# Sixteen of 128 first keys taken out of three tiles' expert gathers and worked out densely

## The chip, the cores and the metric

One core of one Trainium2 chip. The time is the device time in microseconds of one launch. Before: 2917.52 us, the median of three runs (2913.64 to 2918.01).

## The reference

A hybrid attention block over 1024 tokens of width 1024, and behind it a PEER layer, which is what matters here. For each token, 8 heads score 128 first keys and 128 second keys, take the best 16 of each, form the 256 sums, and keep the best 16. Each names one of 128 × 128 = 16384 experts; an expert is a row `u` and a row `v` of 1024 floats.

```python
top_s, pos = lax.top_k(cand_s, PEER_TOPK)
idx = jnp.take_along_axis(cand_i, pos, axis=-1)      # i1 * 128 + i2
g = jax.nn.softmax(top_s.astype(jnp.float32), axis=-1)
u = expert_u[idx]
act = jax.nn.gelu(jnp.einsum('thkd,td->thk', u, tb).astype(jnp.float32), approximate=False)
coef = (g * act).astype(tb.dtype)
return jnp.einsum('thk,thkd->td', coef, expert_v[idx])
```

Then the residual sum and a last RMSNorm. Everything is float32. The expert number is `i1 * 128 + i2`, so all experts of the sixteen highest first keys (112 to 127) have numbers from 14336 on: they are the last 2048 rows of the table.

## The kernel before

The 1024 tokens are eight tiles of 128, worked in eight **blocks** b = 0 to 7. Block b does the experts of tile b, and beside it all other work of tile b + 1 (attention, output product, norm, queries, keys, top-k), and, in blocks 0 to 4, parts of the stick-breaking attention of later tiles. Blocks 5 and 6 have no such attention, block 7 no next tile.

**Experts of a block.** 128 gathers, one for each of the 128 (head, rank) slots, in 64 groups of two (`GRP` = 2, `NG` = 64). A gather is an indirect DMA on GpSimd (L763): 128 rows of `experts`, a row being `u` and `v` side by side, 8192 bytes, into one of nine slots of `r_uv` (64 tokens × 2 ranks over the 128 partitions). The slot order is `SLOT`; a gather waits until TensorE has used the slot's former row (`rows_used`). For every row:

- VectorE multiplies `u` with the normed token and sums (L1437, "the dot"), in place over the `u` half; once a group it builds the gated identity (L1421) from the softmax gates.
- ScalarE applies Gelu to the group's dots (L1020) and writes the gated identity times that over the first 64 columns of the row (L1023).
- TensorE multiplies this 128 × 64 diagonal with `v` in two halves of 512 columns (L1877) and sums over the whole block in PSUM banks 0 and 1. That frees the slot.

All four engines run their own list of instructions, written out by hand: in each engine's `experts_of(b, ...)` the loop runs over the groups n, and tables `at`, `at_own` say which step of the next or of the own tile stands behind which group. VectorE has the largest of these lists: in groups 1 to 25 the second four heads' top-k of the own tile (`top`, `pick`, `gate`, `routed`), in groups 2 to 17 the attention steps of the next tile (`rope`, `mask`, `norm`, `h2`, `hn`), in 27 to 52 the first four heads' top-k of the next tile. A `look` step has three instructions over 800 columns (L1206, L1208, L1209).

TensorE's steps for the next tile are in groups 1 to 29: L1773 is the output product, L1795 the queries, L1816 the keys. L1684 spreads a gain vector over PSUM by eight products (`spread_gain`).

**Finish of a tile.** In block b + 1, group 0: VectorE adds the experts' sum to `h2cur` (`add_rows`, L1399). Group 1: ScalarE's square with its sum, Ln and Exp (L1012, L788, L789; the table is loaded at L784). Group 3: VectorE's Newton step (L1060 to L1064) and the scaling (L1409), then SyncE stores the tile. Group 7: VectorE copies the next residual row into `h2cur` (L1450). After group 63 of block 7 the same chain stands at the end of the kernel.

**SyncE** issues all other DMAs in one list: stored and loaded pieces of the projections, attention keys and values, the rows of the next tile, the finished tiles. From block 5 on it has little to do.

Of the kernel before, what the change touches and what calls it, by code (L numbers as in the profile page):

```python
# [26 lines left out]
P = 128  # L27
# [189 lines left out]

C_ID, C_TRI, C_ONES, C_M01, C_MNEG, C_PERM = (P * i for i in range(6))
# [30 lines left out]
def block_program(nc, x, meta, w_chunks, w_v, consts, rope_cs, w_out, sinks, w_query, keys_t, experts, out):  # L249
    with ExitStack() as ctx:  # L250
# [36 lines left out]
        keysT = grid(sb("keysT", PH * NKEYS), PH)  # L287
# [23 lines left out]
        stream_chunk = grid(sb("stream_chunk", D)[:, :], DC)  # L311
# [72 lines left out]

        def chunk_home(c):

            return wchunk[CHUNK_HOME[c]]
# [31 lines left out]
        lvm_dram = scratch("lvm_dram", [META, PAIRS, P])  # L419

# [42 lines left out]
        hs_in = sem("hs_in")  # L463
        gid_ready = sem("gid_ready")
# [8 lines left out]
        passed = {}  # L473
        for name in ("pe", "act", "dve", "pool", "sp"):
            passed[name] = sem("passed_" + name)
# [13 lines left out]
        def _(sp_eng):  # L489
# [108 lines left out]

            def piece_moves(n0, n1):
# [15 lines left out]
            def late_moves(b, first):  # L615
# [18 lines left out]
                for n, (u, last) in enumerate(LATE_LOADS[first]):  # L634
# [4 lines left out]
                    if n == 2:  # L639
                        if pairs == 2:  # L640
                            if b < STREAM_BLOCKS:
                                stored(pieces_by(at))
                            load_queries(1)

                        gate(e, "sp", qT_done, PH * b + 2 * PH)
                    if n >= LKB:

                        gate(e, "sp", lw_used, ub + LATE_LOADS[first][n - LKB][1] + 1)
# [23 lines left out]
            def store_block(b):  # L672
                e.wait_ge(out_ready, b + 1)
                e.dma_start(out[P * b:P * b + P, :], h2cur[:, :]).then_inc(out_done, 16)

            for b in range(NT):
                if b:
# [3 lines left out]
                    e.wait_ge(out_done, 16 * b)  # L681
# [10 lines left out]
                elif b + 2 < NT:  # L692

                    gate(e, "sp", mix_done, 4 * b + 8)
                    load_window(b + 2)
            for h in range(2):
                e.wait_ge(out_ready, NT + h)
                cols = slice(D // 2 * h, D // 2 * h + D // 2)
                e.dma_start(out[P * (NT - 1):P * NT, cols], h2cur[:, cols]).then_inc(out_done, 16)
# [4 lines left out]
        def _(pool):  # L704
# [40 lines left out]
            def gathers_of(b, late=None):  # L745
                for k in range(K):
# [14 lines left out]
                    elif SLOT[G] in (2, 3):  # L761
                        gate(pool, "pool", proj_summed, NP)
                    g.indirect_dma_start(uv[:, SLOT[G], :], None, experts,  # L763
                                         bass.IndirectOffsetOnAxis(idx[b % 2][:, k:k + 1], 0)
                                         ).then_inc(rows_in[SLOT[G]], 16)
# [10 lines left out]
        def _(act):  # L776
# [229 lines left out]

            def finish(b):
# [4 lines left out]
                link(a.activation(qT_v[:, :], h2cur[:, :], ACT.Square, accum_out=r4[:, 0:1]))  # L1012
# [4 lines left out]
            def experts_of(b, more, late=None):  # L1017
                for n in range(NG):
# [8 lines left out]
                    if n == 1 and b:  # L1027
# [3 lines left out]
                    if n in (own_at if b else own_first):  # L1031
                        tile_step((own_at if b else own_first)[n], b)
                    if late is not None and (late_units(late, n - WEIGHTS[late]) or late_units(late, n - LOGS)):
# [13 lines left out]
        def _(dve):  # L1047
# [166 lines left out]
            def tile_step(step, t):  # L1214
# [30 lines left out]
                elif step == "pT":  # L1245
                    for i in range(2):
# [35 lines left out]
                elif step == "hn":  # L1282
                    dve.wait_ge(h2_squared, t + 1)
                    polish(r3[:, 1:2], r3[:, 0:1], D)
                    dve.wait_ge(gain_spread, max(1, 2 * t))
# [23 lines left out]
                elif step[0] == "routed":  # L1309
# [7 lines left out]
                    spread(gates[t % 2], gn, TOPK * h0, TOPK * h1).then_inc(routed, 1)  # L1317
# [25 lines left out]
                elif step[0] == "look":  # L1343
                    h = step[1]

# [49 lines left out]
            def add_rows(b):  # L1395

                dve.wait_ge(rows_used, K * b + K + NB)
                hg = h2cur[:, :].rearrange("p (a n) -> p a n", a=2)
                v.tensor_tensor(hg, ps[:, 0:2, :], hg, ALU.add).then_inc(h3_ready, 1)  # L1399

            def finish(b):

                dve.wait_ge(h3_squared, b + 1)
                polish(r4[:, 1:2], r4[:, 0:1], D)
                dve.wait_ge(gain_spread, 2 * b + (3 if b < NT - 1 else 2))
                hg = grid(h2cur[:, :], 2)
                for h in range(2 if b == NT - 1 else 1):
                    part = slice(h, h + 1) if b == NT - 1 else slice(0, 2)
                    v.scalar_tensor_tensor(out=hg[:, part, :], in0=hg[:, part, :], scalar=r4[:, 1:2],  # L1409
                                           in1=ps[:, 4 + part.start:4 + part.stop, :], op0=ALU.mult, op1=ALU.mult  # L1410
                                           ).then_inc(out_ready, 1)

# [567 lines left out]
```

## Time and profile before

| | |
|---|---|
| median of three runs | 2917.52 us |
| profiled execution, span | 2918.2 us (0.7 above the median) |
| busy: PE, DVE, POOL, ACT | 2207.9, 2182.3, 1308.8, 1144.8 us |
| moved by DMA | 1155.22 MB, mean 396 GB/s |
| of it by the gathers' queue | 1073.81 MB |
| mean granted TensorE clock | 0.880 |

The blocks by the first dot of each (start of L1437's instruction 0, 128, 256 ...): block 0 from 175.0, block 1 from 546.1, then 905.6, 1264.5, 1598.6 (block 4), 1933.4, 2261.1, 2586.7 (block 7), and the last dot ends at 2907.5.

How to read it: times are microseconds from the first instruction. PE is TensorE, PEld its weight loads, DVE VectorE, ACT ScalarE, POOL GpSimd, SP SyncE. A group of instructions is named by its line, and "idle before" is the time its engine stood idle just before it, with what ended that. DMA share is the mean busy share of the sixteen DMA engines. Busy matmuls overlap, so their busy sum is less than count times mean.

### The profile page before, as it was taken

What the parts mean: (1) busy time and instruction counts of PE and PEld (TensorE: products, weight loads), DVE (VectorE), ACT (ScalarE), POOL (GpSimd) and SP (SyncE); (2) the same over time, 40 slices, a digit from 0 to 9 for tenths busy, and PEclk for the clock granted to TensorE, in tenths of its full rate; (3) what the DMA queues carried; (4) which work ended last, traced back from release to release, by engine and by line L of the source; (5) the groups of instructions that cost most, each with busy time, mean ns of one, the idle gap of its engine ahead of it and who ended that gap; (6) DMA issues with size and microseconds to landing.
All of it is one profiled execution on the core that took longest, in us unless ns stands there. A gap on an engine that the chain in (4) does not pass through costs nothing.

```text
span 2918.2 us, 30160 instructions
## 1 busy us (share of the span) xinstructions
PE 2207.9 (76%) x9182; PEld 944.6 (32%) x9182; DVE 2182.3 (75%) x5506; ACT 1144.8 (39%) x2673; POOL 1308.8 (45%) x1126
## 2 busy tenths in 40 slices
PE   9988888788887988867877777867755775565555
PEld 7564532345333453323322232212311231111111
DVE  4179887786867867689786988779776987668555
ACT  3523277433563335632575327733212321121111
POOL 0024355443554445544565445644444444444442
PEclk9999998999999999988998899988877898777778
DMA  8279999999999999999999999999999999999997
GB/s 324 91 290 406 382 404 420 407 412 389 416 387 419 413 392 411 391 415 420 420 419 408 421 419 403 416 417 418 421 409 422 420 403 420 417 422 406 422 421 322
DMA packets 189328, 1155.22 MB, mean 396 GB/s; under 512 B 23072, under 2 KB 40416, under 8 KB 57712
## 3 DMA queue, kind: packets, MB, share of 16 engines
q0 software_dynamic: 147456, 1073.81, 89.6%
q1 hardware_dynamic: 41712, 79.49, 7.3%
q8 instruction: 74, 1.21, 0.2%
q14 instruction: 86, 0.70, 0.1%
HBM read 1138.21 MB, written 15.01 MB: 395 GB/s over the span
## 4 chain that ended last, share of the span: by engine, by line
DMA 34%; PE 26%; DVE 24%; ACT 9%; issue 5%; POOL 1%; another core or an unknown queue 0%; ACTq 0%; DVEq 0%; SPq 0%; POOLq 0%
DMA r_uv<-in_experts,r_wk 34%; PE ps L1877 12%; DVE r_uv L1437 11%; PE ps L1547 4%; ACT r_uv L1023 2%; PE ps L1795 2%; PE ps L1541 2%; ACT L1020 2%; DVE r_wk L1208 1%; DVE r_wk L1206 1%; DVE r_wk L1209 1%; ACT L784 1%; PE ps L1773 1%; POOL r_uv L763 1%; PE ps L1563 1%
## 5 line engine op out<-in xcount | busy, mean ns | idle before, releaser
L763 POOL DMA_INDIRECT r_uv<-in_experts,r_wk x1024 | 1202.8, 1175 | 1416.7 <-PE ps L1877 1207.6
L1877 PE MATMUL ps<-r_uv 128*64 128x512 f32 x4096 | 1229.8, 733 | 679.0 <-ACT r_uv L1023 662.6
L1437 DVE CUSTOM_DVE_ANT_0 r_uv<-r_uv,hnrep 128x1024 f32<-128x1024 f32 x1024 | 1255.9, 1241 | 555.9 <-DMA r_uv<-in_experts,r_wk 541.0
L1877 PEld LDWEIGHTS ps<-r_uv 128*64 128x64 f32 x4096 | 290.2, 157 | 1424.2 <-ACT r_uv L1023 955.8
L1020 ACT ACTIVATE r_wk<-r_wk 128x2 f32<-128x2 f32 x512 | 103.8, 203 | 1455.5 <-DVE r_wk L1437 1426.4
L1023 ACT ACTIVATE r_uv<-gid,r_wk 128x64 f32<-128x64 f32 x684 | 200.6, 340 | 11.6 <-ACT r_wk L1020 0.2
L1020 ACT ACT_TABLE_LOAD x138 | 177.1, 1283 | 2.4
L784 ACT ACT_TABLE_LOAD x117 | 150.1, 1283 | 6.1 <-PE ps L1753 1.8
L1547 PE MATMUL ps<-r_uv,stream_chunk 128*128 128x256 f32 x560 | 134.0, 394 | 4.7 <-DMA stream_chunk<-in_w_chunks 4.7
L1795 PEld LDWEIGHTS ps<-r_wk,r_wq 128*128 128x128 f32 x1024 | 120.2, 193 | 37.4 <-issue 36.8
L1795 PE MATMUL ps<-r_wk,r_wq 128*128 128x128 f32 x1024 | 129.3, 281 | 0.3 <-ACT r_wk L940 0.3
L1547 PEld LDWEIGHTS ps<-r_uv,stream_chunk 128*128 128x128 f32 x560 | 106.2, 195 | 50.6 <-issue 36.9
L1557 PE MATMUL ps<-r_wk 64*128 64x256 f32 (+2 forms) x384 | 110.0, 419 | 4.3 <-DMA r_wk<-lkv_dram 1.9
L1421 DVE TENSOR_TENSOR gid<-cst,r_wk 128x128 f32<-128x128 f32 x342 | 106.4, 311 | 0.0
L1023 ACT ACTIVATE r_uv<-cst,r_wk 128x64 f32<-128x64 f32 x340 | 99.7, 340 | 5.7
L714 POOL TENSOR_TENSOR r_wk<-r_wk 128x512 f32<-128x512 f32 (+1 forms) x64 | 85.0, 1328 | 31.3 <-PE ps L1569 30.6
L1563 PE MATMUL ps<-r_wk,cst 128*128 128x512 f32 (+2 forms) x184 | 99.0, 621 | 0.0
L1437 DVE DVE_READ_ACCUMULATOR2_ANT r_wk<- 128x1 f32 x1024 | 83.5, 81 | 0.0
L712 POOL COPY r_wk<-r_wk 128x256 f32<-128x256 f32 x32 | 21.0, 657 | 134.7 <-PE ps L1566 106.0
L1557 PEld LDWEIGHTS ps<-r_wk 64*128 64x128 f32 (+1 forms) x384 | 45.8, 178 | 84.5 <-issue 83.8
L1569 PE MATMUL ps<-r_wk,cst 128*128 128x512 f32 (+2 forms) x152 | 72.0, 556 | 0.0
L1208 DVE TENSOR_TENSOR r_wk<-r_wk 128x800 f32<-128x800 f32 (+1 forms) x65 | 63.5, 978 | 2.2
(181 smaller groups left out, 2206.2 us busy)
## 6 DMA issues: line engine op xcount, KB each, us to landing
r_uv<-in_experts,r_wk POOLq DMA_INDIRECT x1024
stream_chunk<-in_w_chunks SPq DMA_DIRECT2D x30, 512.0 KB
r_wk<-lkv_dram SPq DMA_DIRECT2D x36, 256.0 KB
r_uv<-in_x SPq DMA_DIRECT2D x8, 512.0 KB, 10.6
r_wo<-in_w_chunks SPq DMA_DIRECT2D x8, 512.0 KB, 11.4
r_wk<-in_x SPq DMA_DIRECT2D x8, 512.0 KB
r_wo<-in_w_out SPq DMA_DIRECT2D x8, 512.0 KB, 9.5
r_wq<-in_w_query SPq DMA_DIRECT2D x8, 512.0 KB, 6.4
```

Source lines behind the costliest of these rows:

```text
L763: g.indirect_dma_start(uv[:, SLOT[G], :], None, experts, bass.IndirectOffsetOnAxis(idx[b % 2][:, k:k + 1], 0)).then_inc(rows_in[SLOT[G]], 16)
L784: a.preload_act_table_set("natural_log_exp_and_others")
L1020: link(a.activation(actv[:, GRP * n:GRP * n + GRP], actv[:, GRP * n:GRP * n + GRP], ACT.Gelu))
L1023: a.activation(uv[:, SLOT[K * b + k], 0:HALF], gid[(NG * b + n) % 3][:, k % GRP, :], ACT.Copy, scale=actv[:, k:k + 1]).then_inc(diag_ready, 1)
L1208: link(v.tensor_tensor(eq, eq, ci[:, h, 0:among].unsqueeze(1).unsqueeze(1).to_broadcast(every), ALU.mult))
L1421: v.tensor_tensor(gid[m % 3][:, :, :], ident64.unsqueeze(1).to_broadcast([P, GRP, HALF]), gates[b % 2][:, GRP * n:GRP * n + GRP].unsqueeze ...
L1437: v.tensor_tensor_reduce(uv[:, slot, 0:D], uv[:, slot, 0:D], hnrep[:, k % GRP, :], 1.0, 0.0, ALU.mult, ALU.add, actv[:, k:k + 1]).then_inc ...
L1547: last = t_.matmul(piece_sums(i, width), w[:, c, :], tokens, start=c == 0, stop=c == DC - 1)
L1557: t_.matmul(bank(u, r, c0, r0=r0)[:, h, :], k[rows, 0:r], q[rows, c0:GW], start=opens, stop=False, skip_group_check=True).then_inc(lz_half ...
L1563: last = t_.matmul(bank(u, r, c0), negtri[0:r, 0:r], sp[0:r, :, c0:GW], start=False, stop=not own and rest == GW, skip_group_check=True)
L1795: last = t_.matmul(into, wq[:, c, P * h:P * h + P], hnT[:, c, :], start=c == 0, stop=c == DC - 1)
L1877: last = t_.matmul(ps[HALF * j:HALF * j + HALF, i, :], uv[:, slot, 0:HALF], uv[:, slot, D + 512 * i:D + 512 * i + 512], start=n == 0, stop ...
```

## The change

For tiles 4, 5 and 6 (`DENSE`), the experts of the last sixteen first keys (`NA` = 16, numbers from `CUT` = 14336) leave the gathers and are worked out for all 384 tokens at once.

- **Gathers** of blocks 4 to 6 get a bound of `CUT - 1`: a row beyond it isn't an error and is left out. The slot keeps what it held. The gates of such rows are set to 0 (one more small VectorE instruction in `routed`), and the dots of these blocks write their products elsewhere (`spent`, the unused `stage` and `stream_chunk`) so that a slot's `u` half stays finite.
- **Kept for later**, by SyncE: the normed columns of tiles 4 to 6 (`hn_dram`, 0.5 MB each), their expert numbers and gates (`route_dram`, 2 × 64 KB each), and instead of the finished tiles 4 and 5 the partial sums (`part_dram`). The finish of tiles 4 to 6 (squares, Newton step, scaling, store) moves to the end of block 7. Tile 6's partial sum stays in `h2cur`; tile 7 stays in `hs`.
- **Block 6:** SyncE loads the columns again and, through four buffers, sixteen blocks of `u` (512 KB each, transposed on the host: `dense_u`). From group 30, a half block a group, TensorE forms 128 experts × 384 tokens (eight products a block), and ScalarE applies Gelu (`late_act`). In groups 56 to 63 the three tables of expert number and gate are split into first and second key and turned.
- **Block 7, groups 0 to 33:** for each token, the gates are put in the place of their expert: a mark "second key equals column" (128 × 128) times gates by first key (128 × 16), one product a token. VectorE makes the marks of tiles 5 and 6 eight tokens at a time (32 units), ScalarE those of tile 4 four tokens at a time (32 steps of four squares and a Relu); VectorE multiplies the counted gates into `late_act`, twelve times.
- **Block 7, groups 35 to 60:** SyncE loads sixteen blocks of `v` (the first four already in block 6), TensorE sums all into six PSUM banks, 96 products of 512 columns. Groups 61 to 63: the three tiles are added, squared, scaled, and stored ahead of tile 7.
- Six pairs of idle products near the end (L1883) go.

```diff
+NA = 16
+CUT = (NKEYS - NA) * NKEYS
+DENSE = (4, 5, 6)
+DB = 4
+UNIT = 8
+STEP = 4
+SHARE = 16
+DOTS_AT = 30
+TABLE_SPLIT_AT, TABLE_TURN_AT, TABLE_KEEP_AT = (56, 58, 60), 62, 63
+ACT_STEPS_AT = {h: h for h in range(P // STEP)}
+DVE_UNITS_AT = {u: u for u in range(2 * NU_OF)}
+ACT_TIMES_AT = {COUNTED // STEP * (m + 1) + 1: m for m in range(P // COUNTED)}
+DVE_TIMES_AT = {CHUNK_U * m + CHUNK_U + 1: m for m in range(2 * NU_OF // CHUNK_U)}
+SUMS_AT = [35 + 13 * v // 16 for v in range(2 * NA)]
+CLOSE_ADD_AT, CLOSE_SQUARE_AT, CLOSE_SCALE_AT = 61, 62, 63
...
@@ SyncE
+            def load_dense(n):
+                if n >= DB:
+                    if n - DB < NA:
+                        e.wait_ge(dots_done, n - DB + 1)
+                    else:
+                        e.wait_ge(dense_used, n - DB - NA + 1)
+                a = n % NA
+                if n < NA:
+                    e.dma_start(dense[n % DB].rearrange("p (c k) -> p c k", c=DC), dense_u[a]).then_inc(chunk_in[n % DB], 16)
+                else:
+                    e.dma_start(dense[n % DB], experts[CUT + P * a:CUT + P * a + P, D:2 * D]).then_inc(chunk_in[n % DB], 16)
...
@@ GpSimd
+                    if b in DENSE:
+                        g.indirect_dma_start(uv[:, SLOT[G], :], None, experts,
+                                             bass.IndirectOffsetOnAxis(idx[b % 2][:, k:k + 1], 0),
+                                             bounds_check=CUT - 1, oob_is_err=False
+                                             ).then_inc(rows_in[SLOT[G]], 16)
...
@@ ScalarE
+                for k in range(STEP):
+                    last = a.activation(mark[:, k, :], key_iota, ACT.Square, scale=-1.0, bias=turned_of[0][:, 1, at + k:at + k + 1])
+                link(last)
+                a.activation(mark, mark, ACT.Relu, scale=-2.0, bias=1.0).then_inc(act_marked, 1)
...
@@ VectorE
+                v.tensor_tensor(mark, key_iota.unsqueeze(1).to_broadcast([P, UNIT, P]),
+                                turned_of[i][:, 1, k0:k0 + UNIT].unsqueeze(2).to_broadcast([P, UNIT, P]), ALU.is_equal)
+                link(v.tensor_tensor(share, block_iota.unsqueeze(1).to_broadcast([P, UNIT, NA]),
+                                     turned_of[i][:, 0, k0:k0 + UNIT].unsqueeze(2).to_broadcast([P, UNIT, NA]), ALU.is_equal))
+                v.tensor_tensor(share, share, turned_of[i][:, 2, k0:k0 + UNIT].unsqueeze(2).to_broadcast([P, UNIT, NA]), ALU.mult
+                                ).then_inc(dve_marked, 1)
...
+                            if b in DENSE and k >= 2:
+                                dve.wait_ge(dotted, K * b + k - 1)
-                            v.tensor_tensor_reduce(uv[:, slot, 0:D], uv[:, slot, 0:D], hnrep[:, k % GRP, :], 1.0, 0.0,
+                            v.tensor_tensor_reduce(spent[k % 2] if b in DENSE else uv[:, slot, 0:D], uv[:, slot, 0:D],
+                                                   hnrep[:, k % GRP, :], 1.0, 0.0,
...
@@ TensorE
+            def count_tokens(bank, at, mark, share):
+
+                for k in range(mark.shape[1]):
+                    last = t_.matmul(ps[:, bank, NA * (at + k):NA * (at + k) + NA], mark[:, k, :], share[:, k, :],
+                                     start=True, stop=True)
+                return last
...
+                for j in range(ND):
+                    last = t_.matmul(ps[:, 2 + 2 * j + i, :], late_act[:, a_, P * j:P * j + P],
+                                     dense[n % DB][:, 512 * i:512 * i + 512], start=a_ == 0, stop=a_ == NA - 1)
```

## Rows read from the trace of the kernel before

**Rows 1.** The page: DMA share by slices, and the two large queues.
```profile
DMA  8279999999999999999999999999999999999997
...
q0 software_dynamic: 147456, 1073.81, 89.6%
q1 hardware_dynamic: 41712, 79.49, 7.3%
```

**Rows 2.** The page's groups: the gathers and the dots.
```profile
L763 POOL DMA_INDIRECT r_uv<-in_experts,r_wk x1024 | 1202.8, 1175 | 1416.7 <-PE ps L1877 1207.6
...
L1437 DVE CUSTOM_DVE_ANT_0 r_uv<-r_uv,hnrep 128x1024 f32<-128x1024 f32 x1024 | 1255.9, 1241 | 555.9 <-DMA r_uv<-in_experts,r_wk 541.0
```

**Rows 3.** The chain that ended last, from 2880 us on: start, length, what.
```profile
2883.65 3.50 PE ps L1877 x8
...
2891.14 15.15 DMA r_uv<-in_experts,r_wk
...
2906.32 1.22 DVE r_uv L1437
...
2908.46 1.99 PE ps L1877 x8
...
2911.73 1.16 ACT r_wk L1012 x2
...
2912.91 0.30 ACT small L788
```

**Rows 4.** Stretches of block 4: first half, groups 4 to 7, second half.
```profile
1598.60:1766.40 167.80, 123.85 (x560) 53.61 (x558) 145.87 (x405) 57.99 (x155) 75.33 (x64) 0.89 1.01 420
1619.10:1642.80 23.70, 14.16 (x57) 4.53 (x54) 22.87 (x66) 9.55 (x31) 9.86 (x8) 0.71 1.01 421
1766.40:1933.40 167.00, 128.96 (x468) 40.98 (x467) 129.54 (x266) 114.01 (x204) 103.15 (x82) 0.92 1.00 409
```

**Rows 5.** Stretches of blocks 5 and 6, halves.
```profile
1933.40:2100.40 167.00, 124.28 (x550) 54.05 (x548) 146.01 (x405) 52.63 (x147) 76.44 (x64) 0.87 1.01 420
2100.40:2261.10 160.70, 92.19 (x258) 20.91 (x256) 109.14 (x242) 28.10 (x99) 69.56 (x64) 0.73 1.01 416
2261.10:2426.60 165.50, 120.93 (x552) 52.15 (x548) 145.55 (x406) 52.45 (x147) 79.53 (x64) 0.90 1.01 413
2426.60:2586.70 160.10, 88.44 (x256) 20.43 (x256) 108.97 (x241) 28.10 (x99) 70.55 (x64) 0.77 1.01 419
```

**Rows 6.** Stretches of block 7, halves.
```profile
2586.70:2748.80 162.10, 94.53 (x266) 22.93 (x268) 120.23 (x310) 32.19 (x105) 74.88 (x64) 0.73 1.00 414
2748.80:2907.50 158.70, 96.90 (x292) 24.03 (x288) 85.21 (x159) 24.48 (x93) 64.16 (x58) 0.80 0.96 401
```

**Rows 7.** Groups by form in block 7: busy us, mean ns of one, idle before.
```profile
L1023 ACT ACTIVATE r_uv<-gid,r_wk 128x64 f32<-128x64 f32 x86 | 25.2, 340 | 1.4
...
L1421 DVE TENSOR_TENSOR cst<-cst,r_wk 128x128 f32<-128x128 f32 x21 | 6.1, 292 | 0.0
L1684 PE MATMUL ps<-cst 128*128 128x128 f32 x32 | 4.1, 281 | 0.0
L1206 DVE TENSOR_TENSOR r_wk<-cst,r_wk 128x800 f32<-128x800 f32 x4 | 4.0, 992 | 0.1
...
L784 ACT ACT_TABLE_LOAD x2 | 2.6, 1283 | 0.1
...
L1409 DVE SCALAR_TENSOR_TENSOR h2cur<-h2cur,small,ps 128x1024 f32<-128x1024 f32 x1 | 1.3, 1281 | 0.5 <-PE ps L1684 0.5
L1450 DVE COPY h2cur<-r_wk 128x1024 f32<-128x1024 f32 x1 | 0.7, 687 | 0.0
```

**Rows 8.** Groups by form from 1600 to 2500 us.
```profile
L1773 PE MATMUL ps<-r_wo,oa 128*128 128x512 f32 x48 | 22.2, 605 | 0.0
...
L1101 DVE SCALAR_TENSOR_TENSOR r_wk<-ps,r_wk 128x512 f32<-128x512 f32 x14 | 9.5, 681 | 0.0
L852 ACT ACTIVATE r_wk<-r_wk 128x512 f32<-128x512 f32 x14 | 8.8, 630 | 0.4
```

More of the change, by code:

```diff
@@ L215, with dense_of, finished_before, gain_number @@
 TILES = [0, 1, NT] + list(range(2, NT))
+NA = 16
+CUT = (NKEYS - NA) * NKEYS
+DENSE = (4, 5, 6)
+ND = len(DENSE)
+DT = ND * P
+DB = 4
+UNIT = 8
+NU_OF = P // UNIT
+CHUNK_U = 512 // (NA * UNIT)
+DOT_BANKS = (4, 5)
+ACT_BANKS, DVE_BANKS = (6, 3), (7, 2)
+STEP = 4
[4 more added lines that the diff above has]
+DVE_UNITS_AT = {u: u for u in range(2 * NU_OF)}
+ACT_COUNTS_AT = {h + 1: h for h in range(P // STEP)}
+ACT_SHARES_AT = {4 * j: j for j in range(P // SHARE)}
+DVE_COUNTS_AT = {u + 1: u for u in range(2 * NU_OF)}
+COUNTED = CHUNK_U * UNIT
+ACT_TIMES_AT = {COUNTED // STEP * (m + 1) + 1: m for m in range(P // COUNTED)}
+DVE_TIMES_AT = {CHUNK_U * m + CHUNK_U + 1: m for m in range(2 * NU_OF // CHUNK_U)}
+SUMS_AT = [35 + 13 * v // 16 for v in range(2 * NA)]
+CLOSE_ADD_AT, CLOSE_SQUARE_AT, CLOSE_SCALE_AT = 61, 62, 63
+def dense_of(t):
+    return DENSE.index(t)
+def finished_before(t):
+    return sum(x not in DENSE for x in range(t))
+GAINS = []
+for _b in range(NT):
+    if _b and _b - 1 not in DENSE:
+        GAINS.append(("out", _b - 1))
+    GAINS.append(("ffn", _b + 1 if _b else 0))
+    if _b == 0:
+        GAINS.append(("ffn", 1))
+GAINS = GAINS[:-1] + [("out", NT - 1)]
+def gain_number(kind, t):
+    return GAINS.index((kind, t)) + 1
 C_ID, C_TRI, C_ONES, C_M01, C_MNEG, C_PERM = (P * i for i in range(6))
@@ L1011, in finish @@
                 act.wait_ge(h3_ready, b + 2)
-                link(a.activation(qT_v[:, :], h2cur[:, :], ACT.Square, accum_out=r4[:, 0:1]))
+                rows = hs if b == NT - 1 else h2cur[:, :]
+                link(a.activation(qT_v[:, :], rows, ACT.Square, accum_out=r4[:, 0:1]))
                 if b < NT - 1:
@@ L1678, in late_weigh, with dense_dots @@
                            j == 2 * g + 1, j == NT)
-            def spread_gain(at):
+            def dense_dots(h):
+                a_, half = h // 2, h % 2
+                if h == 0:
+                    pe.wait_ge(late_in, 16 + 16 * ND)
+                    pe.wait_ge(qT_kept, 2 * NT)
+                if half == 0:
+                    pe.wait_ge(chunk_in[a_ % DB], 16 * (a_ // DB + 2))
+                    if a_ >= 2:
+                        pe.wait_ge(dots_kept, a_ - 1)
+                w = dense[a_ % DB].rearrange("p (c k) -> p c k", c=DC)
+                for c in range(4 * half, 4 * half + 4):
+                    last = t_.matmul(ps[:, DOT_BANKS[a_ % 2], 0:DT], w[:, c, :], late_hnT[:, c, :], start=c == 0, stop=c == DC - 1)
+                if half:
+                    last.then_inc(dots_done, 1)
@@ new lines, in turn_tables @@
+            def turn_tables():
+                pe.wait_ge(key_kept, 4 * NT)
+                for i in range(ND):
+                    pe.wait_ge(tables_split, i + 1)
+                    for place, which in ((0, 0), (1, 2), (2, 1)):
+                        last = t_.transpose(ps[:, (6, 7, 3)[i], P * place:P * place + P], table_of[i][:, which, :], ident)
+                    last.then_inc(tables_turned, 1)
+            def count_tokens(bank, at, mark, share):
[3 more added lines that the diff above has]
+                return last
```

292 lines of the change are left out of this document (259 added, 33 removed).

## The prediction

> **What bounds the kernel now.** I read the page first. The slices and the queue table [rows 1] say that the DMA engines are never free between the second and the last of forty slices, and that the gathers alone (1024, 128 rows of 8192 bytes each, 144 packets: 128 rows and sixteen semaphore writes) take 89.6% of them. That is 0.896 × 2918.2 = 2615 us, 2.553 us a gather, 0.319 us a row on its engine (128 rows over 16 engines: eight each), 2.435 us a MB. Everything on the hardware queue is 79.5 MB in 7.3%, 213 us, 2.68 us a MB. Next the groups [rows 2]: GpSimd spends 1.2 us on a gather and sits idle for a free slot, released by TensorE's expert product; VectorE's dots wait for the gathers to land. Then the end of the chain of waits [rows 3]: a gather takes 15 us from issue to landing although its transfer is 2.6 us, so it queues behind others. That queue is the reserve: an engine may fall behind by that much before the DMA engines run dry. Last the stretches by block [rows 4, 5, 6]; the columns are start:end, length, busy time of PE, PEld, DVE, ACT and POOL (instruction counts), TensorE's clock, DMA share and GB/s. A block is cut at its first dot; the middle is group 32 of 64. DMA share is 1.01 in both halves of blocks 4 to 6. So a byte saved is time saved, as long as VectorE keeps up, and there the rows warn: in the first half of blocks 4 to 6 it is busy 146 of 166 to 168 us, and in one stretch of four groups 22.87 of 23.70, which is 96.5% and as full as I take it to get.
>
> **What the gathers save.** Counting the reference's own indices for tiles 4, 5 and 6, the rows with a first key of 112 or more are 2108, 1887 and 1836 of 16384 each: 5831 in all. If the engines shared the saving evenly it would be 5831/16 × 0.319 = 116 us. But a row belongs to a partition and a partition to an engine, a gather has landed only when all sixteen have finished, and only nine slots are in flight; so the engine with most rows left sets the pace of a block. The trace doesn't show which partitions go together. With eight neighbouring partitions to an engine, the fullest keeps 923, 937 and 934 of its 1024 rows: 278 rows less, 88.7 us. With every sixteenth partition it is 922, 953 and 954: 243 rows, 77.5 us. Bounds 77 and 116; I take 89, since a fixed assignment is what equal eights per gather look like.
>
> On this the Trainium skill, "DMA: Bandwidth & Descriptors", section "The descriptor swizzle", says that in a transfer over 128 partitions each engine serves two runs of four partitions that are 32 apart. By that rule the fullest engines keep 909, 945 and 946 rows, which would make the term 86.8 us and the sum 2 us worse; no row here shows the assignment.
>
> **What the dense part moves.** Sixteen blocks of the u half and sixteen of the v half at 0.524 MB are 16.78 MB in rows of 4 KB; at the gathers' 2.435 us a MB, 41 us. Smaller pieces: normed columns out and back 3.15 MB, routes 0.79, counts 0.07, two partial tiles out and back 2.10; 6.1 MB at 2.68 make 16 us. Of these 57 us the partial tiles' return (1.05 MB, 3 us) falls into a stretch where, as below, the DMA engines have time. So +54, of which some 32 in the second half of block 6 (all u blocks and four v blocks: SyncE comes to them only after block 7's mix and queries, group 27) and 16 in the second half of block 7.
>
> **VectorE in block 7** is the term that I think matters most. All the marks and gate shares sit in groups 0 to 32. Durations [rows 7]: L1206 has the same form as a mark (two broadcasts, is_equal), 992 ns for 800 columns; L1421, also two broadcasts, 292 ns for 128. That is 1.04 ns a column: 1.23 us for 1024, 0.42 for 256. A unit is 1.23 + 2 × 0.29 = 1.81 us, 32 of them 58 us; eight pairs of gate shares for ScalarE's tile 8 × 2 × 0.42 = 7 us; ten of the twelve products fall in this half, 0.68 us each by L1101 [rows 8], 7 us. Removed: tile 6's finish (L1409, 1.28, and some five instructions on one column) and the copy to h2cur (L1450, 0.69), 2.8 in all by estimate. So 120.2 + 72 - 2.8 = 189 us of work [rows 6] in a half that took 162. At 96.5% this needs 196 us: VectorE falls 34 us behind. The reserve takes some: issue to landing is 15 us, and a gather that finds the queue empty must still take its 2.6 us and the issue around it, 5 to 7 in all by my estimate, so 8 to 10. The DMA engines stand idle for 34 - 9 = 25 us, and nothing afterwards gives that back, since the second half is bound by DMA. Bounds: 189 without gaps and a reserve of 10, 17 us; no reserve, 34.
>
> **VectorE in blocks 4 to 6.** With 89 to 92% of the rows the DMA pace of a first half falls to 147 to 154 us, VectorE needs 146/0.965 = 151. The heavy stretch (groups 4 to 7, 23.7 us against 18.3) and the picks of groups 16 to 20 eat a lag of 6 to 9 us, about the reserve. I charge 3 us a block, 9; bounds 0 and 15. The extra multiply by "index under the bound" is two small instructions a tile, 1 us, in the same charge. The second waits of the dots cost nothing: they ask for the dot before the one that is running.
>
> **ScalarE and TensorE.** A mark step is four squares and a Relu over 512 columns: 4 × 0.4 (L1023 takes 0.34 for 64 columns) + 0.6 (L852), 2.3 us a group; ScalarE is busy 32 of 162 us there now, so covered. TensorE: 128 dense dots over 384 columns, between 0.28 (L1684, 128 columns, rows 7) and 0.60 us (L1773, 512, rows 8), so 0.5: 64 us on 88 of 160 in block 6's second half, which itself grows to 176. Counts: 384 products of 16 columns with 128 x 128 weights; by L1684 0.28 at most, in a row perhaps 0.25, 96 us, on top of 94.5 of 162. Sums: 96 × 0.6 = 58 us in the second half. All covered if the clock is at its upper level; the clock was granted at 0.73 there [rows 6], and eight expert products take 3.5 us at the lower level and 2.0 at the upper [rows 3]. So 0 here, and a rival below. GpSimd: a compare per row, nothing by 1.2 of 2.5 us; upper bound in a rival. The waits that SyncE takes on for routes_ready stand until group 25 of the block; behind them are only the next stores.
>
> **The end.** In the last groups ScalarE does three squares with their Ln and Exp (1.2 + 0.3 and some 0.2, 5 us in all [rows 3]) and two table loads of 1.28 (L784), against a group's pitch of 5: about 4 us late for the last Gelu. VectorE's three scalings (2.1 us each) lie partly in the 2.9 us that it waits between its last dot and the end of the last products, longer by ScalarE's delay. +5; bounds 2 and 12.
>
> **Sum**, against the profiled execution (span 2918.2, 0.7 us above the median of the three runs, 2917.5): -89 + 54 + 25 + 9 + 5 = +4, so 2922 us. The saved bytes are given back by the dense loads and by VectorE in block 7. A measurement of this kernel can tell some 0.2% (6 us) from no change, so this is no change. The case's own range, by the bounds above, is 2898 to 2946.
>
> **Rivals.** (1) *The saving is shared evenly*: rows left out don't leave holes in one engine's list, and VectorE's gaps are smaller. 116 instead of 89 and 22 instead of 34 for VectorE give 2883 to 2900, say 2893. For it: nothing ties a row to an engine in the trace. Against: eight rows an engine in each gather. 0.28. (2) *TensorE becomes the bound in block 7*: it is in order, and behind the counts and sums stand the expert products that free the slots. At the upper level its work is 64 × 2.0 + 96 + 58 = 282 us in a block of some 360; if it grows as the clock falls, it fills the block at 282/360 = 0.78 granted, and that is the point from which it decides. Price 20 to 50 us beyond the above, 2957. Against it: a busier engine should be granted more, as in block 4 (0.89 against 0.73). 0.16. (3) *The bound doesn't do what it says*: a row beyond it still costs a read or a packet of like length, or GpSimd's 1.2 us a gather double. Then the +93 us of the other terms stand less a little: 2980 to 3010. No row shows a gather with a bound. 0.08. The forecast 0.48.
>
> **Numbers.** Faster by over 0.2% (under 2911.7): rival 1 and 0.2 of the forecast's case: 0.38. Within: a third of that case, whose middle lies at the edge of this band: 0.16. Slower: the rest of it and rivals 2 and 3: 0.46. The range for 8 in 10 runs from 2880 to 2966; it leaves out rival 3 and the outer ends of the first two.
>
> **What would show it.** In blocks 4 and 5 gather packets fewer by 12.9 and 11.5%, block lengths about 302 to 308, block 6 near 330, DMA share under 1.00 though the queue is never empty (engines waiting for the fullest). A DMA share of 1.01 with shorter blocks would be rival 1. In block 7's first half VectorE busy 189 of 190 to 196 us and gathers' wait for landings gone; block 7 at 355 to 365 us. If instead its dots still wait for DMA there, my largest charge is wrong, and the kernel is faster by it. TensorE waiting for nothing and L1877's wait gone would be rival 2; packets of 8192 bytes unchanged in number, rival 3.

## The result, and the profile after

The changed kernel takes 2995.55 us (median of four runs, 2983.9 to 2997.63) against 2916.22 for the kernel before in the same comparison: a ratio of 1.027, 95% interval 1.0248 to 1.0292. I had forecast 2922 with a range of 2880 to 2966, so it is slower, outside the range, and by far more than the +4 us of my sum. All stretches and block lengths below are read from one profiled execution of each kernel, and all times are of one execution unless a median or a ratio is given. The profiled execution has a span of 2991.7 us, 73.5 longer than before.

The page of the changed kernel: busy slices, the clock and DMA share, then the two large queues [rows 1].

```profile
PE   9988898788878888777886888777567788898997
PEclk9999998899989999989897899889778889766799
DMA  8289999999999999999999999999999999977897
...
q0 software_dynamic: 147456, 1026.06, 85.2%
q1 hardware_dynamic: 51888, 102.38, 9.2%
```

The gathers moved 47.8 MB less and the hardware queue 22.9 MB more, both as counted ahead. The number of gather packets is the same as before: a row beyond the bound leaves a packet of 4 bytes (22,215 packets of 4 bytes in place of 16,384, which is 5831 more, the rows that I had counted). But three slices near the end (the 36th to the 38th), where the DMA engines were full before, are at 7 and 8 tenths, and there TensorE's row is at 8 and 9 and its clock row at 6 and 7.

The stretches show where, cut at the first dot of groups 0 and 32 as in [rows 4, 5, 6]; the columns are start:end, length, busy time of PE, PEld, DVE, ACT and POOL, TensorE's clock, DMA share, GB/s. Blocks 4, 5, 6 and 7, two halves each:

```profile
1596.30:1759.10 162.80, 125.84 (x556) 54.44 (x554) 145.04 (x406) 57.03 (x153) 81.96 (x64) 0.87 0.95 374
1759.10:1918.90 159.80, 131.02 (x474) 41.81 (x470) 129.41 (x266) 115.33 (x206) 110.94 (x83) 0.93 0.98 382
1918.90:2080.00 161.10, 122.19 (x532) 53.15 (x532) 143.46 (x401) 48.41 (x141) 81.81 (x65) 0.86 0.97 383
2080.00:2227.40 147.40, 86.23 (x254) 20.31 (x256) 108.49 (x242) 28.09 (x99) 83.42 (x64) 0.75 1.00 407
2227.40:2389.10 161.70, 122.22 (x528) 52.10 (x524) 143.59 (x401) 48.56 (x141) 76.34 (x64) 0.86 0.98 384
2389.10:2570.80 181.70, 154.30 (x529) 63.89 (x529) 111.21 (x253) 36.08 (x118) 79.39 (x64) 0.94 0.98 390
2570.80:2803.80 233.00, 208.47 (x974) 126.40 (x976) 180.76 (x425) 85.68 (x259) 72.64 (x64) 0.67 0.82 305
2803.80:2973.90 170.10, 160.09 (x508) 59.66 (x504) 88.94 (x165) 26.41 (x95) 66.70 (x57) 0.96 0.97 397
```

| | before | after | forecast |
|---|---|---|---|
| block 4 | 334.8 | 322.6 (-12) | 302 to 308 |
| block 5 | 327.7 | 308.5 (-19) | 302 to 308 |
| block 6 | 325.6 | 343.4 (+18) | about 330 |
| block 7 | 320.8 | 403.1 (+82) | 355 to 365 |
| last dot to the end | 10.7 | 17.8 (+7) | +5 |

Block 7's first half alone is 71 us longer. VectorE's busy time there is 181 us (I had worked out 189), in 233. TensorE is busy 208 of 233 at a granted clock of 0.67 (a mean of its two levels, 1.2 and 2.4 GHz; before the change it was 0.73 here, with TensorE busy 95 of 162), and the DMA engines stand a fifth of the time. The groups by form in block 7:

```profile
L2243 PE MATMUL ps<-r_uv 128*64 128x512 f32 x512 | 172.5, 810 | 41.0 <-ACT r_uv L1214 36.2 <-DVE h2cur L1610 4.8
...
L2042 PE MATMUL ps<-r_wq,r_wo 128*128 128x512 f32 x192 | 89.3, 606 | 0.0
L2006 PE MATMUL ps<-r_wk,keysT 128*128 128x16 f32 x256 | 39.2, 297 | 0.0
...
L2006 PE MATMUL ps<-r_wk,oa 128*128 128x16 f32 x256 | 37.6, 290 | 0.0
...
L2006 PE MATMUL ps<-r_wk,stream_chunk 128*128 128x16 f32 x128 | 22.8, 314 | 0.0
...
L2006 PE MATMUL ps<-r_wk,stage 128*128 128x16 f32 x128 | 20.8, 297 | 0.0
...
L1643 DVE TENSOR_TENSOR oa<-r_wo 128x1024 f32<-128x1024 f32 x16 | 19.5, 1222 | 21.0 <-PE ps L2006 21.0
L1643 DVE TENSOR_TENSOR keysT<-r_wo 128x1024 f32<-128x1024 f32 x16 | 19.5, 1222 | 26.7 <-PE ps L2006 26.7
```

L2006 is the counting: 39.2 + 37.6 + 22.8 + 20.8 = 120 us. L2042 is the sums. The counts say something that I had overlooked: 384 count products stand in 768 records and 96 sums in 192. Here a float32 product leaves two. VectorE's marks took 1.22 us, as worked out, and waited for TensorE: the wait had turned round.

### The profile page after: what moved, and what is told of

The parts are those of the page before. It is cut to its first block, busy times and chain, and to the rows that moved or that the text cites. A ratio compares the mean times of both kernels' runs of the same rounds, so it can differ in the third digit from the quotient of the medians.

```text
span 2991.7 us, 33624 instructions
## 1 busy us (share of the span) xinstructions
PE 2450.1 (82%) x10339; PEld 1128.7 (38%) x10339; DVE 2251.5 (75%) x5650; ACT 1206.2 (40%) x2848; POOL 1351.9 (45%) x1126
## 4 chain that ended last, share of the span: by engine, by line
PE 37%; DVE 24%; DMA 21%; ACT 8%; issue 7%; POOL 2%; SPq 1%; DVEq 0%; POOLq 0%; ACTq 0%
DMA r_uv<-in_experts,r_wk 20%; PE ps L2243 16%; DVE r_uv L1712 7%; PE ps L1844 4%; PE ps L2006 3%; PE ps L2139 2%; PE ps L2161 2%; ACT r_uv L1214 2%; PE ps L2042 2%; ACT L1211 2%; PE ps L1838 2%; DVE r_wk L1405 1%; DVE r_wk L1407 1%; DVE r_wk L1408 1%; DVE stream_chunk L1712 1%
## 5 line engine op out<-in xcount | busy, mean ns | idle before, releaser
L2243 PE MATMUL ps<-r_uv 128*64 128x512 f32 x4096 | 1192.6, 713 | 494.1 <-ACT r_uv L1214 476.7
L925 POOL DMA_INDIRECT r_uv<-in_experts,r_wk x640 | 758.2, 1185 | 982.1 <-PE ps L2243 838.1
L1712 DVE CUSTOM_DVE_ANT_0 r_uv<-r_uv,hnrep 128x1024 f32<-128x1024 f32 x640 | 785.0, 1244 | 327.7 <-DMA r_uv<-in_experts,r_wk 322.3
L2243 PEld LDWEIGHTS ps<-r_uv 128*64 128x64 f32 x4096 | 282.8, 153 | 1143.1 <-ACT r_uv L1214 666.2
L920 POOL DMA_INDIRECT r_uv<-in_experts,r_wk x384 | 490.4, 1277 | 461.2 <-PE ps L2243 312.6
L1712 DVE CUSTOM_DVE_ANT_0 stream_chunk<-r_uv,hnrep 128x1024 f32<-128x1024 f32 x192 | 236.7, 1233 | 101.1 <-DMA r_uv<-in_experts,r_wk 100.8
L1712 DVE CUSTOM_DVE_ANT_0 stage<-r_uv,hnrep 128x1024 f32<-128x1024 f32 x192 | 236.0, 1229 | 57.6 <-DMA r_uv<-in_experts,r_wk 53.5
L1990 PE MATMUL ps<-r_wq 128*128 128x384 f32 x256 | 93.0, 507 | 20.9 <-DMA r_wq<-in_dense_u 20.9
L1860 PE MATMUL ps<-r_wk,cst 128*128 128x512 f32 (+2 forms) x184 | 103.6, 646 | 0.3 <-POOL r_wk L870 0.2
L2042 PE MATMUL ps<-r_wq,r_wo 128*128 128x512 f32 x192 | 89.3, 606 | 0.0
```

Source lines behind the costliest of these rows:

```text
L920: g.indirect_dma_start(uv[:, SLOT[G], :], None, experts, bass.IndirectOffsetOnAxis(idx[b % 2][:, k:k + 1], 0), bounds_check=CUT - 1, oob_i ...
L925: g.indirect_dma_start(uv[:, SLOT[G], :], None, experts, bass.IndirectOffsetOnAxis(idx[b % 2][:, k:k + 1], 0)).then_inc(rows_in[SLOT[G]], 16)
L1712: v.tensor_tensor_reduce(spent[k % 2] if b in DENSE else uv[:, slot, 0:D], uv[:, slot, 0:D], hnrep[:, k % GRP, :], 1.0, 0.0, ALU.mult, ALU ...
L2042: last = t_.matmul(ps[:, 2 + 2 * j + i, :], late_act[:, a_, P * j:P * j + P], dense[n % DB][:, 512 * i:512 * i + 512], start=a_ == 0, stop ...
L2243: last = t_.matmul(ps[HALF * j:HALF * j + HALF, i, :], uv[:, slot, 0:HALF], uv[:, slot, D + 512 * i:D + 512 * i + 512], start=n == 0, stop ...
```

## The experiments

**Is it the bound on the gathers, and what limits it?** The kernel before with the bound alone:

```diff
+                    if b in DENSE:  # 4, 5, 6
+                        g.indirect_dma_start(..., bounds_check=14336 - 1, oob_is_err=False)
...
-                            v.tensor_tensor_reduce(uv[:, slot, 0:D], ...
+                            v.tensor_tensor_reduce(spent[k % 2] if b in DENSE else uv[:, slot, 0:D], ...
```

> The kernel before, with the bound on the gathers of blocks 4 to 6 and the dots of those blocks written elsewhere, and nothing else; the experts of the last sixteen first keys are left out there (stale rows stand in their place). In the changed kernel blocks 4 and 5, which hold hardly any dense work, took 322.6 and 308.5 us against 334.8 and 327.7. If that is all the bound can give, blocks 4, 5, 6 take about 321, 307, 307 here, some 52 us less in all, 2866 us. If only the fullest DMA engine set the pace (my term of the sum), 89 us less, 2829; if the saving were shared evenly and nothing else bound, 116 less, 2802. If the small pieces that are stored in blocks 4 and 5 had cost the difference, the blocks come out at 300 to 303.

The median is 2856.41 us, a ratio of 0.9777 (0.9757 to 0.9796). The stretches of blocks 5 and 6, two halves each:

```profile
1922.60:2085.10 162.50, 125.04 (x552) 53.87 (x548) 144.74 (x406) 52.61 (x147) 78.92 (x64) 0.87 0.96 378
2085.10:2232.30 147.20, 86.83 (x256) 20.35 (x256) 108.86 (x242) 28.10 (x99) 79.47 (x64) 0.75 1.00 408
2232.30:2390.50 158.20, 125.15 (x550) 55.49 (x548) 144.69 (x406) 52.67 (x147) 79.99 (x63) 0.86 0.98 394
2390.50:2534.80 144.30, 85.94 (x258) 19.80 (x256) 108.61 (x242) 28.10 (x99) 82.81 (x66) 0.76 1.00 400
```

Blocks 4, 5 and 6 take 321.8, 309.7 and 302.5 us: 54 less than before in all, where my term was 89. This profiled execution, 2865.37 us, is the slowest of the four of this kernel. By the ratio the bound gives 65 us (60 to 71), so 54 is a low reading of what it is worth. The small stores in blocks 4 and 5 cost nothing that shows: these two blocks take 631.5 us here and 631.1 in the changed kernel.

The same kernel with the bound at 8192, half of all rows:

> As the run with the bound alone, but the bound in the middle of the table, so that about half of the rows are left out in blocks 4 to 6 (their part of the output is left out). The DMA work of such a block halves to some 165 us, so what is left is the pace of the other engines. If VectorE's and TensorE's own order bounds a block already with an eighth left out, the first halves hardly shrink further: 150 to 160 us each, whole blocks 4 about 300, 5 and 6 about 280. If DMA was still the bound, the first halves fall well below 140.

2781.92 us. The stretches of blocks 5 and 6, two halves each:

```profile
1904.10:2061.20 157.10, 123.08 (x550) 53.43 (x548) 144.56 (x406) 52.54 (x147) 80.93 (x64) 0.87 0.72 229
2061.20:2179.30 118.10, 71.50 (x258) 18.61 (x256) 107.06 (x241) 28.10 (x99) 78.79 (x64) 0.88 0.79 266
2179.30:2334.40 155.10, 118.77 (x548) 52.95 (x548) 144.42 (x405) 52.53 (x147) 83.02 (x65) 0.90 0.71 231
2334.40:2449.90 115.50, 73.05 (x258) 18.86 (x256) 106.35 (x243) 28.10 (x99) 77.98 (x63) 0.86 0.80 267
```

With half of the rows gone a first half still takes 155 to 157 us, with VectorE busy 144.5 of that. One eighth less had brought them from 165 to 168 down to 158 to 163: about half of all there was. The second halves of these two blocks fall to 116 and 118.

**Does the fullest DMA engine set the pace?** Two kernels leave out the same number of rows, one eighth, chosen by partition. A constant of 32768 is added to the index of certain partitions in blocks 4 to 6:

```diff
-                        last = v.tensor_copy(to, from_)
+                        last = v.tensor_scalar(to, from_, cst[HALF * j:HALF * j + HALF, C_OFF:C_OFF + 1], None, ALU.add)
...
+    c[:, C_OFF] = np.where(np.isin(s[:, 0] % HALF, [0, 4, 8, 12, 16, 20, 24, 28]), 32768, 0)
```

> The kernel before, with rows left out by their partition and not by their key: in blocks 4 to 6 the partitions 0, 4, ..., 28 and 64, 68, ..., 92 are sent beyond the bound, one eighth of all rows (their part of the output is left out). If a partition belongs to a DMA engine by runs of four partitions 32 apart, each engine loses exactly one of its eight rows in every gather, and the second halves of blocks 5 and 6, where DMA share was 1.01, go from 160.7 and 160.1 us to 141 to 143. If engines take eight neighbours, four of them lose two rows and others none, and the halves stay at 158 to 161. If rows are dealt out anew after the bound, 141 to 143 as well.

The second kernel has `[0, 1, 2, 3, 32, 33, 34, 35]` in that list.

> As the run before it, with the same number of rows left out, but the partitions 0 to 3, 32 to 35, 64 to 67 and 96 to 99. If each DMA engine serves two runs of four that are 32 apart, two engines have nothing left and fourteen all of theirs: the second halves of blocks 5 and 6 stay at 158 to 161 us although an eighth of the bytes is gone, and DMA share falls to 0.88. If rows are dealt out anew, or the engines share one limit, 141 to 143.

Blocks 5 and 6 of the first (its stretches end at 2503.8, which is where block 7 begins), then of the second:

```profile
1907.00:2063.00 156.00, 121.77 (x550) 54.16 (x548) 144.67 (x405) 52.80 (x147) 78.72 (x63) 0.88 0.98 394
2063.00:2203.10 140.10, 80.78 (x258) 19.44 (x256) 108.16 (x241) 28.10 (x99) 95.50 (x66) 0.81 1.01 414
2203.10:2363.00 159.90, 123.57 (x552) 53.25 (x548) 144.86 (x405) 52.76 (x147) 80.75 (x64) 0.87 0.96 379
2363.00:2503.80 140.80, 83.50 (x256) 20.08 (x256) 107.98 (x243) 28.10 (x99) 88.88 (x64) 0.78 1.01 415
```

```profile
1928.30:2094.80 166.50, 121.33 (x552) 53.02 (x548) 145.90 (x405) 52.40 (x147) 79.21 (x64) 0.90 0.89 371
2094.80:2255.40 160.60, 89.59 (x254) 20.93 (x256) 109.14 (x242) 28.10 (x99) 77.70 (x64) 0.73 0.89 369
2255.40:2420.70 165.30, 126.96 (x552) 55.27 (x548) 145.76 (x406) 52.38 (x147) 77.60 (x64) 0.87 0.88 361
2420.70:2581.30 160.60, 91.67 (x254) 20.76 (x256) 108.97 (x241) 28.10 (x99) 79.27 (x66) 0.73 0.90 372
```

The same rows, the same bytes, and 2836.52 us against 2913.80. Taken from every engine alike, the second halves fall to 140 and 141; taken from two engines, they stay at 160.6 with a DMA share of 0.89, and the eighth is for nothing. The Trainium skill, "DMA: Bandwidth & Descriptors", section "The descriptor swizzle", says for one transfer to 128 partitions that each engine writes two runs of four partitions, 32 apart, and both sets were chosen by that. These runs agree, in an indirect gather too. The two layouts that my prediction worked with fall: eight neighbours to an engine, or every sixteenth partition, would have taken the first set from some engines and left others all their rows. The second halves of the two-engine kernel also show that the other engines did not speed up when two were idle. In the first halves even the even choice leaves 156 and 160 us, at or just above the 155 to 157 that stay with half of the rows gone, so there the other engines' order was most of the limit.

In the kernel with the bound alone the second halves of blocks 5 and 6 took 147.2 and 144.3. With the rows counted ahead, the fullest engine alone (945 and 946 of 1024 rows) would give 148 and an even share 142, so those halves lie between and don't tell the two apart; the pair of kernels here does.

**What does the dense part cost alone?** The changed kernel with `bounds_check=NEXP - 1`, which no row exceeds:

> The changed kernel with a bound that no row exceeds: every row is fetched, the gates of the last sixteen first keys are still 0, the dense part is whole. It tells the price of the dense part alone. If both parts add up, it takes the changed kernel's time and what the bound gave, about 2994 + 50 = 3044 us, blocks 4 and 5 back at 335 to 337 and 328 to 330, block 7 unchanged at 403. If the bound gives nothing in block 6, because TensorE and the late loads set its pace there, block 6 stays at 343 and the time is 3026.

3054.39 us. Blocks 4 and 5 take 337.9 and 329.9, block 6's second half 197.8, block 7's halves 240.0 and 170.2. The two parts add up within the spread of single runs. It is 61 us above the changed kernel's profiled run: blocks 4 to 6 take 58 more (the bound alone had taken 54 off them), block 7's first half 7 more, and the blocks ahead of these 4 less. Block 7's first half takes 233 to 241 us in three kernels whose work there is alike; what that varies with stays open.

**Block 7: TensorE or VectorE?** Two edits of the changed kernel, one for each:

```diff
-                for k in range(mark.shape[1]):
+                for k in (mark.shape[1] - 1,):
                     last = t_.matmul(ps[:, bank, ...
```

> The changed kernel with one product of each set of four or eight tokens in block 7's counting, 64 in place of 384 (the other tokens' share of the dense part is left out). If TensorE is the bound of block 7's first half, that half falls from 233 us to VectorE's own need, about 181/0.965 = 188, and the time by 40 to 45 us. If VectorE is the bound, it stays above 220. The clock granted in this half tells whether the narrow products were what kept it at 0.67.

```diff
-                v.tensor_tensor(mark, key_iota.unsqueeze(1).to_broadcast([P, UNIT, P]), ...
+                v.tensor_tensor(mark[:, 0:1, :], key_iota.unsqueeze(1).to_broadcast([P, 1, P]), ...
```

> The changed kernel with VectorE's marks made for one token of eight (1.0 us less in each of 32 units, 32 us of VectorE's work in block 7's first half; the counts of the other tokens are worked out from what stood there). If TensorE is the bound, the half stays at 225 to 233 us. If VectorE is, it falls to about 200.

Block 7's first half with few counts, then with few marks:

```profile
2565.50:2755.20 189.70, 114.28 (x372) 40.31 (x374) 179.65 (x424) 84.79 (x258) 74.65 (x64) 0.71 0.93 365
```

```profile
2562.40:2790.90 228.50, 209.33 (x972) 128.78 (x974) 150.90 (x425) 85.66 (x259) 67.40 (x64) 0.66 0.82 311
```

Few counts: 2944.34 us, and the half at 189.7, near VectorE's own need as worked out (188). Few marks: 30 us less of VectorE's work, and the half only 4.5 us shorter, less than such halves differ by; 2982.01. So TensorE is the bound of this half, by 43 us beyond VectorE, and VectorE stands behind it by 28 beyond the 162 of before. In the first of these runs the clock stayed at 0.71, with a TensorE that was idle 40% of the time; that doesn't say yet why it was low in the changed kernel.

**The low clock.** Every count product four times as wide, with the same weights:

```diff
-                    last = t_.matmul(ps[:, bank, NA * (at + k):NA * (at + k) + NA], mark[:, k, :], share[:, k, :], ...
+                    last = t_.matmul(grid(ps[:, bank, 0:4 * NA], 4), mark[:, k, :], share[:, k, :].unsqueeze(1).to_broadcast([P, 4, NA]), ...
```

> The changed kernel with every count product four times as wide (64 columns for 16, the same weights; the counted numbers land in the wrong place). More work for TensorE, the same number of products. If narrow products are what keeps TensorE's clock at 0.67 in block 7's first half, the clock rises well above 0.8 and the half gets no longer than 233 us, perhaps shorter. If it is the waits and not the width, the clock stays at 0.65 to 0.7 and the half grows by up to 384 times some 0.05, 20 us.

```profile
2566.90:2780.90 214.00, 169.80 (x976) 105.05 (x976) 180.88 (x424) 85.26 (x259) 73.11 (x64) 0.85 0.87 331
```

More work, and the half is 19 us shorter, at 214.0, with the clock at 0.85; 2966.68 us in all, 17 below the fastest of the changed kernel's four runs. TensorE's busy time fell from 208 to 170. At 16 columns the engine was busy 89% of the stretch, and the clock was granted at 0.67 all the same. Why the wide products are granted more no run shows. Of the 43 us beyond VectorE, 19 come back with the clock alone and 24 stay at 0.85 (one execution each).

**Fewer passes.** Marks and gate shares in bfloat16 (a mark is 0 or 1, the gates are rounded):

```diff
-        marks = [view.rearrange("p (k n) -> p k n", k=UNIT) for view in
+        marks = [view[:, 0:UNIT * P // 2].bitcast(BF16).rearrange("p (k n) -> p k n", k=UNIT) for view in
```

> The changed kernel with marks and gate shares of the counting in bfloat16 (marks are 0 or 1, gates are rounded; nothing left out). If TensorE's counting is what holds block 7's first half, one pass in place of several brings it near the run with few counts: the half at 190 to 200 us, the time at 2945 to 2955. If the count of products and their waits matters and not their length, the half stays above 220.

```profile
2566.30:2753.20 186.90, 103.76 (x612) 31.74 (x614) 179.23 (x426) 84.83 (x258) 71.65 (x64) 0.72 0.93 370
```

2941.93 us. TensorE's records in the half fall from 974 to 612 (a bfloat16 product leaves one: the counting has 384 records for 384 products), its busy time to half, and the stretch is VectorE's: 179 of 187.

**Block 6.** In the changed kernel TensorE stood before the first dense block. SyncE's issues there (the second line has the shortest, the middle and the longest of the three in ns), then TensorE, then GpSimd:

```profile
2372.53 18.87 SPq L832 DMA_DIRECT2D r_wq<-hn_dram  x3
L832 SPq DMA_DIRECT2D r_wq<-hn_dram x3: 538/706/17542, 2372.5 to 2373.9; - x3
2391.44 11.42 SPq L710 DMA_DIRECT2D r_wq<-in_dense_u  x4
...
2406.43 4.74 PE L1990 MATMUL ps<-r_wq 128*128 128x384 f32 x8 [20.95 <-DMA r_wq<-in_dense_u]
...
2414.39 0.99 POOL L920 DMA_INDIRECT r_uv<-in_experts,r_wk  x1 [25.85 <-issue]
```

Three DMAs in pieces of 512 bytes hold SyncE for 19 us, nearly all of it in the third: the first two are issued in 0.5 and 0.7 us, the third takes 17.5, and the loads of `u` stand behind it. So it is no fixed price of a DMA or of a piece; SyncE is held once the first 2048 pieces are under way, and on what no run shows. TensorE is in order, so the expert products behind the dense one wait, no slot comes free, and GpSimd issues nothing for 26 us. The edit loads each tile's columns in whole rows and lets TensorE read them with a stride:

```diff
-        late_hnT = grid(late_hnT_v, DC)
+        late_hnT = late_hnT_v.rearrange("p (i c n) -> p c i n", i=ND, c=DC)
...
-                e.dma_start(late_hnT[:, :, P * i:P * i + P], hn_dram[i].rearrange("p (c n) -> p c n", c=DC)
-                            ).then_inc(late_in, 16)
+                e.dma_start(late_hnT_v[:, D * i:D * i + D], hn_dram[i]).then_inc(late_in, 16)
```

> The changed kernel with the three tiles' columns loaded back as rows of 4096 bytes (128 rows a tile in place of 1024 pieces of 512 bytes), kept tile by tile and read by TensorE with a stride. Nothing is left out. SyncE's three issues took 17.5 us and TensorE stood 21 us at group 31 of block 6 for the first dense block. If that issue time is the cause, the stall shrinks by about 15 us and the time with it, to some 2980; if the stall comes from the queries of block 7 being late, under 5 us.

2989.47 us (1.0251, 1.0231 to 1.0271): 6 us below the changed kernel by the medians, but the two intervals overlap, so no gain in the whole is shown. The same rows, by the three issues and then TensorE:

```profile
L832 SPq DMA_DIRECT2D r_wq<-hn_dram x3: 326/432/557, 2370.2 to 2371.1; - x3
2389.28 5.29 PE L1989 MATMUL ps<-r_wq 128*128 128x384 f32 x8 [7.12 <-DMA r_wq<-in_dense_u]
```

The three issues take 1.4 us together, the stall 7 instead of 21, and the half falls from 181.7 to 170.7. The first half of block 7 was 240.8 in this run in place of 233.0, within the spread of that half, so in this execution most of it didn't reach the end.

**Both mends together.**

> The run before it together with the whole rows of the dense part's columns in block 6. Both mends together: block 6's second half near 171 us, block 7's first near 195, the time about 2940. That would still be slower than the kernel before, by what the traffic and VectorE's marks cost: about 0.8%. If mending block 6 only moves the wait into block 7, 2950.

2932.61 us, 1.0068 (1.0046 to 1.0091): 63 us below the changed kernel, with nothing left out (the gates are rounded), and still slower than the kernel before. In its profiled execution, the fastest of six, block 6's second half is 165.3 us, block 7's halves 187.9 and 169.4.

**What is the floor?** All DMAs and waits of the dense part, next to none of its compute (two of eight products of a dot, one count of each set, a third of the sums, one mark in eight on VectorE and one square in four on ScalarE):

> The changed kernel with all its DMAs and waits, but next to none of the dense part's compute: two of eight products of each dense dot, one count of each set, one token's mark of each VectorE unit, one square of each ScalarE step, a third of the sums (that part of the output is left out). It prices the dense part's traffic. If the DMA term of my sum (57 us) was right, it takes the bound alone (2856) plus 57, some 2913, plus 7 for the longer end: 2915 to 2922, and no way of hiding the compute can make the change faster than that. If the traffic finds room beside the gathers, 2880 to 2895, and better hidden compute would make the change pay.

2933.83 us, 1.006 (1.0031 to 1.0089). This is above my 2915 to 2922. Block 6's stall for the first dense block is still in it (TensorE waits 20.7 us for it), and so is part of VectorE's work in block 7's first half (150.6 us, for 120.2 before), so it is no clean floor. Its halves of blocks 6 and 7:

```profile
2390.00:2569.40 179.40, 115.07 (x337) 31.67 (x337) 111.10 (x253) 35.69 (x118) 83.43 (x64) 0.79 0.98 392
2569.40:2740.90 171.50, 106.79 (x371) 38.01 (x372) 150.57 (x424) 57.07 (x163) 75.53 (x64) 0.77 0.97 391
2740.90:2914.90 174.00, 125.36 (x360) 36.19 (x356) 89.70 (x164) 27.72 (x98) 61.63 (x58) 0.84 1.00 413
```

Against the bound alone (144.3, 159.7 and 158.4) that is 35, 12 and 16 us, 63 in all; by the medians this kernel is 77 above the bound alone. So with the loads issued as they are, better hidden compute would hardly have made this change pay: the bound gives 54 to 65 us, and the loads, what is left of the work around them and the later end take it back. The loads in whole rows with next to none of the compute were not run.

## Why the prediction was wrong

By its own steps:

- **What the gathers save, 89.** The mechanism held, though the layout was a guess: a fixed assignment, and the fullest engine sets the pace where DMA is the bound. But 54 us is what the three blocks gave, so this term with the next one, -80 together, should have been -54 (-65 by the ratio of the bound alone).
- **VectorE in blocks 4 to 6, 9 (0 to 15).** This is where those 26 us went. I took 146/0.965 = 151 us as VectorE's need of a first half and let the reserve absorb the lags. The floor is 155 to 157, measured with half the rows gone, and at one eighth less the half takes 158 to 163. I read that as order and DMA being late in turn, which the nine slots don't average; no run separates the two. With all DMA engines relieved alike, 3 × 128 rows or 122 us of each one's work went, and the three blocks took 907 us for 988, 81 less.
- **What the dense part moves, 54.** The bytes were right to the megabyte. Block 6's second half was forecast at 176 and came to 181.7; of this the stall for the first dense block is a part, which I had not looked for: I named SyncE's late start but not how long 3072 pieces hold it. The second half of block 7 got 11 us longer, not 16.
- **VectorE in block 7, 25.** Right as a size, in part by luck: with TensorE out of the way the half takes 187 to 190 us, 25 to 28 more than before. But the work was 181 us and not 189, and at my 96.5% that needs 187 by itself, so the 9 us of reserve that I took off don't show; the two errors cancel. And it wasn't the bound.
- **ScalarE and TensorE, 0.** This is the step that failed, and it is 43 of the 70 us that I was wrong by in all (73.5 against 4 by the spans), most of the rest being the 26 above. I set TensorE at 0 because "all covered if the clock is at its upper level". It failed twice. The counts cost 120 us and not 96; the sums 89 and not 58, the dense dots 93 and not 64. For the last two, where the clock was at 0.94 to 0.96, I had taken the duration of one record for a whole product, of which each leaves two (the 2048 expert products of L1877 stand as 4096 records in the trace of before; so do the ten idle products of L1883, five pairs and not six, as 20). And the clock was granted at 0.67 beside the counts, where the upper level was my condition; 19 of the 43 us came back at 0.85. The condition itself was weak: the half had been granted 0.73 before, and I weighed TensorE against the whole block. By the half, 32 groups at 2.0 and 96 for the counts are 160 us of 187, so that by my own way of reckoning TensorE decides there from 0.86 granted and not from 0.78.
- **The end, 5.** It was 7.
- **Rival 2** is what happened, with its place, its point (below 0.78; granted 0.67) and its price (20 to 50 beyond the forecast; 43). I gave it 0.16 with the argument that a busier engine should be granted more. That did not hold here: TensorE went from 95 of 162 us busy to 208 of 233, and the clock from 0.73 to 0.67. With the same number of products the granted clock was 0.67 at 16 columns and 0.85 at 64. The rival's 2957 was still 38 us low, by the two terms above.
- **Rivals 1 and 3** fell: the even share by the two kernels with rows left out by partition, and the bound does what it says at the price of a 4-byte packet.

## What to carry to other kernels

Where engines work in order over a shared ring of slots, price every engine against the stretch that it shares, not against the block, and add what each must do there to its own floor: a saving of 12% in the bound engine's work shortened the first halves by 3 to 4%, and the other engines' floor there lay only 7% down. Work that is put beside a full stretch is free only if the engine stays free at the clock that it will be granted there; here 384 narrow products were what filled it. And before computing something again to save traffic, set the traffic of the new way against the saving as that engine sees it: 48 MB less in three blocks gave 54 to 65 us, 23 MB more took 63 to 77 with the waits and the rest of the work around them.

## What was not expected of the hardware

- Products four times as wide made the kernel 27 us faster than the changed one's profiled run (2966.7 against 2993.7, one execution of each), with nothing else changed; the granted clock in the stretch went from 0.67 to 0.85.
- A row beyond the bound of a gather leaves a packet of 4 bytes in place of one of 8192; GpSimd's instruction takes 1.28 us with the bound and 1.19 without (means over 384 and 640 gathers).
- Leaving out an eighth of the rows gave 85 us (2836.5 against 2921.9) or, on two engines' partitions, no more than the 8 that single runs differ by.
- Of three DMAs of half a MB in 1024 pieces each, issued one behind the other, the first two held SyncE 0.5 and 0.7 us and the third 17.5 (17.7 and 18.3 in two other kernels with the same issues); in 128 rows each they held it 0.3 to 0.6.
